# Weaving the convolution's norm, the past pages and half of the output projection into the prompt attention, with the value pages on SyncE's queue

## The reference: what is computed

```python
z = h @ W['w_in_even'][e]
q, k, v, fl, a, b = jnp.split(z, cuts, axis=-1)
logf = log_sigmoid(fl + b_forget)
o_fox = fox_attend(e, q, k, v, logf)          # prompt: causal; samples: 8 pages of 128 old tokens each
u = a * sigmoid(b)
xp = concatenate([conv_buf, u], axis=1)
cv = depthwise_conv(xp, conv_w) + conv_b       # 31 taps
cv = silu(_group_norm(cv, 8) * g + b)
out = concatenate([o_fox, cv], axis=-1) @ W['w_out_even'][e]
```

## Time and profile before

| | us |
|---|---|
| median of 3 runs (lowest, highest) | 1930.45 (1929.25, 1932.46) |
| the profiled execution, device time | 1925.21 |
| its span, first to last instruction | 1923.4 |
| PE busy | 1774.2 (92%) |
| DVE busy | 864.9 (45%) |
| ACT busy | 573.5 (30%) |
| POOL busy | 213.7 (11%) |
| mean granted clock of TensorE | 0.942 of 2.4 GHz |

### The profile page before, as it was taken

How to read it: one execution, slowest core, us unless ns; L and a number is a source line. 1 busy time by engine, 2 the same in 40 slices (tenths; PEclk the granted TensorE clock), 3 DMA queues, 4 the chain that set the end, 5 groups by cost and what they waited for, 6 DMA issues and landing times.

```text
span 1923.4 us, 31960 instructions
## 1 busy us (share of the span) xinstructions
PE 1774.2 (92%) x12929; PEld 1549.1 (81%) x12929; DVE 864.9 (45%) x1461; ACT 573.5 (30%) x816; POOL 213.7 (11%) x229
## 2 busy tenths in 40 slices
PE   5899888779899999999899999999968799999997
PEld 3899443327799999999797879799738799999997
DVE  2699346613533232334634637337463533333324
ACT  2422443201442122122333434314331432222223
POOL 1000048600200000000100101101120100000001
PEclk7899668789999999999999999999978999999998
DMA  8463045577434434443231725334742123233321
GB/s 300 139 214 102 2 138 153 175 256 236 147 94 164 149 103 146 144 139 97 66 105 53 224 76 185 121 91 135 263 141 86 58 88 99 77 97 97 89 72 53
DMA packets 288066, 248.82 MB, mean 129 GB/s; under 512 B 9000, under 2 KB 239816, under 8 KB 287951
## 3 DMA queue, kind: packets, MB, share of 16 engines
q1 hardware_dynamic: 262740, 173.97, 29.8%
q0 software_dynamic: 15824, 58.99, 8.6%
q10 hardware_dynamic: 9395, 14.36, 2.1%
HBM read 224.05 MB, written 23.70 MB: 129 GB/s over the span
## 4 chain that ended last, share of the span: by engine, by line
PE 83%; DVE 6%; ACT 3%; POOL 3%; DMA 2%; issue 2%; ACTq 1%; SPq 0%; POOLq 0%; DVEq 0%
PE product L728 60%; PE product L743 5%; PE job L1140 2%; POOL sqa L2094 2%; DMA vp<-in_cache_v 2%; PE job L625 2%; PE job L619 1%; PE job L1123 1%; PE job L917 1%; PE job L658 1%; PE job L893 1%; PE job L1026 1%; PE job L1115 1%; DVE rstd L1591 1%; PE job L1046 1%
## 5 line engine op out<-in xcount | busy, mean ns | idle before, releaser
L728 PE MATMUL product<-H_hi,w_lo 128*128 128x260 f32 x2368 | 674.1, 285 | 3.0 <-ACT gate L1172 2.9
L728 PE MATMUL product<-H_lo,w_hi 128*128 128x260 f32 x2368 | 668.9, 282 | 0.0
L728 PE MATMUL product<-H_hi,w_hi 128*128 128x260 f32 x2368 | 668.4, 282 | 0.0
L728 PEld LDWEIGHTS product<-H_hi,w_lo 128*128 128x128 f32 x2368 | 445.5, 188 | 16.2 <-issue 14.2
L728 PEld LDWEIGHTS product<-H_hi,w_hi 128*128 128x128 f32 x2368 | 446.1, 188 | 0.0
L728 PEld LDWEIGHTS product<-H_lo,w_hi 128*128 128x128 f32 x2368 | 445.9, 188 | 0.2
L1561 DVE TENSOR_TENSOR w_lo<-raw,w_hi 128x1024 fp32r<-128x1024 f32 (+1 forms) x228 | 274.9, 1207 | 169.1 <-ACT w_hi L1172 168.2
L1172 ACT ACTIVATE w_hi<-raw 128x1024 fp32r<-128x1024 f32 (+1 forms) x228 | 234.6, 1037 | 308.2 <-PE product L728 188.9
L728 PE MATMUL product<-G_hi,w_lo 128*128 128x260 f32 x912 | 260.4, 286 | 5.9 <-DVE X L1645 2.5
L728 PE MATMUL product<-G_lo,w_hi 128*128 128x260 f32 x912 | 259.3, 284 | 0.0
L728 PE MATMUL product<-G_hi,w_hi 128*128 128x260 f32 x912 | 259.2, 284 | 0.0
(11 more groups left out here) (319 smaller groups left out, 2139.3 us busy)
## 6 DMA issues: line engine op xcount, KB each, us to landing
spare<-in_ada_w POOLq DMA_DIRECT2D x24, 1024.0 KB, 9.0
raw<-in_w_in_odd SPq DMA_DIRECT2D x48, 512.0 KB, 3.7
raw<-in_w_ffn_gate SPq DMA_DIRECT2D x44, 512.0 KB, 3.8
raw<-in_w_ffn_up SPq DMA_DIRECT2D x44, 512.0 KB, 3.6
kp<-in_cache_k SPq DMA_DIRECT2D x64, 256.0 KB, 2.7
raw<-in_w_ffn_down SPq DMA_DIRECT2D x32, 512.0 KB, 3.3
st<-in_state_ret POOLq DMA_DIRECT2D x28, 512.0 KB, 4.3
out_ret_sample<-st POOLq DMA_DIRECT2D x28, 512.0 KB, 4.5
```

The costliest lines, as they stand in the source:

```text
L728: mm = pe.matmul(Gp[slot][:, c, 0:CH], w[:, j, k, :], x[:, k, cols], start=k == 0 and p == 0, stop=k == kt - 1 and p == 2)
```

## The change

Stages 2, 4, 5 and the convolution's half of stage 6 are put between the 32 steps of the attention. Tables of steps say which piece follows which step (`QB_AT`, `VN_AT`, `KN_AT`, `CM_AT`, `CB_AT`, `V_AT`, `GATHER_AT`, `CONV_OUT_AT`). In detail:

- The rows `cpo`, `cso`, `qs`, the running sums `cum` and `cumT`, the forget logs and the samples' taps go between the input blocks.
- Key pages: three per step instead of two, so that they end with step 21. The samples' softmax is made in two halves of four samples (steps 11 to 15 and 21 to 25).
- The group mean is subtracted by the matmul itself (a constant matrix of identity minus mean), and ACT writes the result and its square; the inverse root is spread with two matmuls of 64 rows each.
- The output projection is made as 8 blocks over the convolution's 512 features (`out_conv`, 24 matmuls each, steps 19 to 26) and 8 over the attention's 512 (`out_even`, 24 each, at the end). N_BLOCKS grows by 8; each block's weights have half the size.
- The values: 16 units of four pages in a ring of three units, laid in the halves of `raw`, `w_hi` that half-size blocks leave free, and in a third place. Two units make one sample; the result goes through a job (`ov`), ACT copies it, and the gather masks the heads through its right operand. All units are issued by SyncE, between the key pages; ScalarE issues none.
- Tiles are laid elsewhere (SS, kp, VN, sq4, lg and others) so that they can live at the same time.

```diff
+V_AT = {17: 0, 19: 1, 21: 2, 23: 3, 27: 4, 29: 5, 31: 6}
+CONV_OUT_AT = {19 + i: i for i in range(8)}
+PER_STEP = 3
...
-    jobs += [(("cm", t, c), "D") for t in range(4) for c in range(2)]
...
+            if x in CM_AT:
+                jobs += [(("cm", CM_AT[x], c), "A") for c in range(2)]
...
+        def value_unit(eng, u, js):
+
+            if u < 2:
+                eng.wait_ge(block_done, N_OUT_EVEN)
+                eng.wait_ge(lo_ready, N_OUT_EVEN)
+            elif u == 2:
+                wait_job(eng, ("cq", 1))
+            elif u % 2 == 0:
+                wait_job(eng, ("ov", (u - 3) // 2))
+            else:
+                eng.wait_ge(v_used, (u - 3) // 2 + 1)
+            for j in js:
+                page(eng, 4 * u + j, cache_v, value_page(u, j), v_unit[u % 3])
...
+            def centred(t):
+                pe.wait_ge(conv_step, 4 * CW)
+                pe.wait_ge(cs_ready, 4)
+                for c in range(2):
+                    bank = open_job(("cm", t, c))
+                    close(pe.matmul(bank[:, 0:CH], con[:, C_CEN:C_CEN + P], CV[:, t, c * CH:(c + 1) * CH],
+                                    start=True, stop=True))
...
+            def group_rstd(t):
+                pe.wait_ge(conv_act, 1)
+                for c in range(2):
+                    bank = open_job(("cb", t, c))
+                    for e in range(2):
+                        mm = pe.matmul(bank[HD * e:HD * e + HD, 0:CH],
+                                       con[0:8, C_ID + 2 * t + e:C_ID + 2 * t + e + 1].broadcast_to((8, HD)),
+                                       CR[:, c * CH:(c + 1) * CH], start=True, stop=True)
+                    close(mm)
...
+            def past_values(b):
+                bank = open_job(("ov", b))
+                pe.wait_ge(samp_dve, 7 + 5 * (b // 4))
+                for u in (2 * b, 2 * b + 1):
+                    pe.wait_ge(v_unit[u % 3], 64 * (u // 3 + 1))
+                    for j in range(4):
+                        mm = pe.matmul(bank[QD * j:QD * j + QD, :], weights_of(b, u % 2 * 4 + j), value_page(u, j),
+                                       start=u % 2 == 0, stop=u % 2 == 1)
+                    if u % 2 == 0:
+                        mm.then_inc(v_used, 1)
+                close(mm)
...
+            def conv_out(i):
+
+                n = N_OUT_EVEN + i
+                if i == 0:
+                    pe.wait_ge(g_ready, 4)
+                pe.wait_ge(lo_ready, n + 1)
+                slots_free(0, conv_base + i - 1)
+                product(n % 4, n % 2, 4, G_hi[:, 4:8], G_lo[:, 4:8]).then_inc(block_done, 1)
...
-            run("out_even", N_OUT_EVEN, 2, KD, G_hi, G_lo, "D")
+            run("out_even", N_OUT_EVEN + KD, 2, 4, G_hi, G_lo, "D")
...
-            act.wait_ge(v_stored, 16 * TB)
-            value_pages(act, 1)
...
-                    for g in range(2 * x, 2 * x + 2):
+                    for g in pages_of(x):
...
+            N = N_OUT_EVEN
+            key_pages(0, 4)
+            out_weights(N, N + 4)
+            key_pages(4, 20)
+            values(0, 2)
+            key_pages(20, 36)
+            values(2, 3)
+            key_pages(36, 52)
+            values(3, 5)
+            key_pages(52, 60)
+            values(5, 7)
+            out_weights(N + 4, N + 6)
+            key_pages(60, 64)
+            values(7, 9)
+            out_weights(N + 6, N + 8)
+            values(9, 11)
+            out_weights(N + 8, N + 12)
+            values(11, 16)
+            out_weights(N + 12, N + 16)
```

More of the change, by code:

```diff
@@ L57 @@
 N_OUT_EVEN = 20
-N_FFN = (28, 160)
-N_ODD = 96
-N_BLOCKS = 228
+N_FFN = (36, 168)
+N_ODD = 104
+N_BLOCKS = 236
 HEAD_BLOCKS = 12
@@ L954, in _ @@
-            turned = open_job("ov")
-            def weights_of(b, g):
-                first = b * PAGES + g
-                return SCP[:].rearrange("p h b g -> p (h b g)")[:, first:first + 31 * 16 + 1:16]
-            def gather(b):
-                pe.wait_ge(vm_ready, b + 1)
-                for t in range(4):
-                    mm = pe.matmul(turned[:, t * NB + b:t * NB + b + 1], vm[:, b % 2, t * P:(t + 1) * P],
-                                   one_col, start=True, stop=True)
-                return mm
@@ new lines, in gather @@
+            def gather(b):
+                bank = open_job(("og", b))
+                wait_emptied(pe, ("ov", b))
+                for t in range(4):
+                    mm = pe.matmul(bank[:, 2 * t:2 * t + 2], vm[:, b % 2, t * P:(t + 1) * P],
+                                   con[:, C_OWN + 2 * t:C_OWN + 2 * t + 2], start=True, stop=True)
+                close(mm)
+            conv_base = runs["out_conv"][1]
+            def conv_out(i):
[5 more added lines that the diff above has]
+                product(n % 4, n % 2, 4, G_hi[:, 4:8], G_lo[:, 4:8]).then_inc(block_done, 1)
@@ L1299, in stage_out @@
                 stage[s] += 1
-            act.wait_ge(cv_ready, 4)
-            stage_out("cpo", CW - 1, 512, A["conv_prompt"][0, 0])
-            stage_out("cso", NB, 512, A["conv_sample"][0, :, CW - 2, :])
-            wait_job(act, "qs")
-            n.up(f(qsn[:], Jp[jobs.bank("qs")][0:NB, :], ACT.Copy), emptied["A"])
-            for b in range(NB):
-                wait_job(act, ("qb", b))
-                n.up(f(QB[:, b, :], Jp[jobs.bank(("qb", b))][:, :], ACT.Copy, scale=FOX_SCALE), emptied["A"])
@@ new lines, in _ @@
+                    if x in EXP_AT:
+                        past_add(EXP_AT[x])
+                    if x in DN_AT:
+                        past_scale(DN_AT[x])
+                    if x in GATHER_AT:
+                        gather(GATHER_AT[x])
+                    if x == SILU_AT + 1:
+                        for t in range(4):
+                            dve.wait_ge(ghi_ready, t + 1)
+                            n.up(minus_hi(G_lo[:, 4 + t, :], CV[:, t, :], G_hi[:, 4 + t, :]), g_ready)
+                        lo(N_OUT_EVEN)
+                        lo(N_OUT_EVEN + 1)
```

821 lines of the change are left out of this document (496 added, 325 removed).

## The result

The changed kernel takes 1911.0 us, the median of 4 runs (1908.0 to 1914.1), beside 1930.9 us (1929.3 to 1932.5) of the kernel before in the same session: ratio 0.9897, 95% interval 0.9878 to 0.9916. It is 20 us faster, where 41 were forecast. Its profiled execution spans 1906.2 us, that of before 1923.4. Medians in this document are of fast runs, which leaves out one run of experiment 10 (its mean clock was 0.638, that of the others 0.943 to 0.949).

A forecast was written before the change was run, and what follows sets the result against it. It took a string of thin, serial stages from 196.8 to 498.2 us, with 51.5 us of TensorE idle, as the bound. Gains of 22.3 us (weave) and 18.8 (projection's rest) made 41, hence 1889 us; range 1848 to 1922.

The forecast's parts named there:

- the clock of the thin matmuls ahead of the blocks: Old attention's part of the weave: granted clock rises from 0.71 to 0.80, cutting 140 us of TensorE work to 124.
- the stall at key page 60: Units 5, 6 ahead of key page 60 in SyncE's queue: 0 us reaches TensorE, covered by some 21 us of work.
- Input projection, start of the weave: Input projection grows by 4.5 us, so the weave starts at 201.3 us instead of 255.2.
- The halves of the group rows: Group rows (L859) become two 64-row halves in the weave: 3.3 us more TensorE work, between 0 and 6.6.
- Value pages: Value pages in the weave wait in units of four: 24.2 us of TensorE work instead of 38.3.
- Projection blocks in the weave: Eight convolution-half blocks of 24 matmuls enter the weave: 8 x 2.97 = 23.8 us of TensorE work.
- SyncE's stalls: Value pages queued ahead of key pages 20, 36, 52, 60 idle TensorE 2, 4, 10, 0 us: 16 in all.
- Handshakes and tail: TensorE idle in the weave: 10 us waiting for banks, copies and softmax turns, 9 us at the last value unit.
- The projection's rest: From the output projection's second half to the mean's matmuls: 29.8 us instead of 48.6, a gain of 18.8.
- rival 2: Loose weave: clock 0.71, idle near today's, 252 us for the weave, 1915 us; chance 0.15.
- Rival 4: No effect: SyncE's queue order lets all four stalls reach TensorE, 43 us instead of 16; 1932 us; chance 0.03.
- Rival 3: Slower: small gaps keep the weave's clock low, losing below a mean of 0.72; 1975 us at 0.6; chance 0.07.

The follow-up runs named there:

- experiment 10: Convolution gates split between steps 16 and 17, on the changed kernel with value pages interleaved and a denser tail: 1870.8 us, ratio 0.9698.
- experiment 2: The interleaved kernel: changed kernel with SyncE's value pages issued singly between key pages instead of in bursts; 1886.3 us, ratio 0.9762.
- Experiment 4: Changed kernel without key-page loads, POOL's 64 products and DVE's 64 sums over them: 1880.9 us, ratio 0.9734.
- experiment 8: Eight extra dense, unused matmuls in each of steps 1 to 16, on top of experiment 2: 1893.7 us, ratio 0.9799.
- experiment 5: Changed kernel with the projection's eight convolution blocks moved out of steps 19 to 26, behind the last head's values: 1921.2 us, ratio 0.9946.
- Experiment 11: Changed kernel with only value units 5 and 6 moved, behind key page 63 instead of 59: 1903.9 us, ratio 0.9857.
- experiment 12: Changed kernel with only value units 3 and 4 moved, behind key page 55 instead of 51: 1900.3 us, ratio 0.9839.
- experiment 9: Changed kernel with all value-page bursts from unit 2 to 6 kept whole but four key pages later in SyncE's queue: 1892.0 us, ratio 0.9804.

## Why the prediction was right or wrong

It forecast 1889 us and got 1911. The sign was right and the time lies in the range, but the gain was half. Two steps failed: the clock of the thin matmuls ahead of the blocks, and the stall at key page 60, put at nothing. The place of the other stalls was right.

- **Input projection, start of the weave.** Forecast 201.3, measured 202.2. Right.
- **The halves of the group rows.** I took 3.3 us; they cost nothing. The 32 matmuls of 64-row tiles (L1014, 6.4 us in the trace) take what the 16 of the earlier trace rows took (6.6). The rule of the Trainium skill, "TensorEngine Tiling (Array Packing)", Key Properties, holds here.
- **Value pages.** Forecast 24.2 us, measured 19.8: units of four pages took 1.04 to 1.10 us where the clock was high (steps 19 to 21) and 1.9 where it was low (step 17), against the 1.51 us of the earlier trace rows.
- **Projection blocks in the weave.** Forecast 23.8, measured 29.1. Six of the eight blocks took 3.1 us each; the second took 4.7 and the fourth, right behind TensorE's wait of 3.1 us at 376.86, took 5.5. In experiment 2, without the stalls, steps 20 to 23 ran at 1.00.
- **Clock: the first step that failed.** "With the idle gaps filled and dense 128-row products between, the clock should be higher": 0.80 for the old attention's part. Everything but value pages and blocks took 150 us where 143 were forecast, at 0.72 up to step 24. Experiment 4 filled the gaps and got 0.75; dense work moved it further (experiment 8). The half of the reason that names dense products holds: from step 20 on the clock was 0.82 and 0.81, and without the blocks 0.59 and 0.70 (experiment 5, 14.6 us for the same work). But the blocks enter at step 19, behind most of the attention, so they could not lift the steps before, at 0.72, 0.64 and 0.67. The earlier trace rows had said so: 0.50 with TensorE 19.86 of 20 us busy. Taken together TensorE's work was 8 us over the forecast.
- **SyncE's stalls: right in sum, wrong in one.** Forecast 2, 4, 10 and 0 us at pages 20, 36, 52 and 60, together 16; the idle times give 1.5, 6.9, 6.7 and 4.9, together 20. The zero was the second step that failed: "PE has blocks 0 to 2 of the projection and unit pair 2, some 21 us". The cover was about right: from unit 5's first page (353.25) to the turn at 376.86 TensorE had 18.7 us of work. What was too short is the chain set against it. I took 13 to 14 us until the first product and 3.8 for three products, 17.5; these end at 370.96, after 17.7. Behind them I had left out DVE, which sums page 62, makes a w_lo, updates X for a block, takes the maximum of a score block, sums page 63 and takes the samples' maximum, until 376.71: 23.5 us in all, 4.8 over the cover, and 4.9 is what TensorE idled. Experiment 11 gives 7 us for this stall alone, and experiment 12 shows that it doesn't hang on the stall before.
- **Handshakes and tail.** Forecast 10 and 9; the interleaved kernel, without stalls, shows 14.3 before step 24 and 10.9 behind it. Idle in all: 44.8, not 35.
- **The projection's rest.** Forecast 29.8, measured 31.0 (at 0.89), and 1.6 us more in the mean's matmuls. I had allowed for this clock loss and not put it in the sum.
- **Sum.** Start 0.9 late, work 8, idle 9.8: 18.7 us at the fox half. Then 1.2 in the half, and 3.9 given back behind it, of which the mean's matmuls are 1.6: 23.8, the difference between the 41 forecast and the 17.2 that the two profiled executions show.
- **Rivals.** What came is rival 2, the loose weave, nearly number for number: clock 0.71 and idle 45 there, 0.73 and 44.8 here, 1915 against 1911. I gave it 0.15. Its reason (every engine carries more per step) is not what experiments 2 and 9 show: the same load per step runs at 25 and 32 us of idle. Rival 4 named the place, SyncE's queue, but at 43 us instead of 20. Rival 3 would need a mean clock under 0.72 over the whole weave; 0.73 was close to it, though the time was not: that sum took the blocks and value pages at full speed as 67 us, so its 0.72 is not the granted clock of the stretch (the forecast's own sum implies 0.87 and names "near 0.8" as its sign). I had also read the earlier trace rows as bearing out that waits lower the clock in the attention; it doesn't, since TensorE is busy 19.86 of 20 us there at 0.50.
- **Signs.** Four of them held: the start at 201, POOL's waits of 12.1 and 13.9 us at pages 36 and 52, TensorE dry behind step 18, and 24.8 us of TensorE's work in the fox half. Missed: TensorE 82% busy instead of over 85, its clock 0.73 instead of 0.8, the wait at page 20 (5.1 us, not 8), the 9.6 us at page 60, key pages done after 173 us instead of 140, the fox half at 446, the mean's matmuls at 477 instead of 457.

The change as it stands wins 20 us of 60 that its idea holds: the order of one queue was worth 25 more, the places of the last values and of four blocks, with their weights, another 16.

## What to carry to other kernels

When two streams share a queue, price the wait at the head of a burst before its issue time, and put the burst behind the entry at which its condition is already true: here that moved 19 us with the same bursts, 15 of them idle time between steps 12 and 23. When you call a stall hidden, follow it past the page that it delays to the last answer that the busy engine needs: the one at key page 60 looked covered until DVE's work behind the products was counted. And expect little clock from filling gaps between thin matmuls (0.72 to 0.75 here); look at what the clock is in a stretch that is already full, and at where the dense products stand, since here they lifted the clock of what stood between them.

## What the runs showed of the hardware

- The clock level follows the kind of work. Eight dense matmuls a step, 24 us in all, gave 0.79 where the other twelve kernels of the weave had 0.67 to 0.73 (experiment 8); steps 20 to 23 had 0.82 with dense blocks and 0.59 without (experiment 5). The Trainium skill, "TensorE: Matmul & The Clock Gate", HAM oscillation, tells of a fall by waiting between short bursts; here and the first pieces above show it low while TensorE is full.
- The same work ran at different clocks. TensorE's matmuls of steps 0 to 11 (240 of them) took 79.0 us at 0.72 in the changed kernel, 83.9 at 0.67 in experiment 2, and 70.6 at 0.80 in experiment 9, which up to key page 36 has the changed kernel's order:
```profile
204.70:282.73 78.03, 70.60 (x240) 37.86 (x239) 47.52 (x103) 34.25 (x86) 54.59 (x53) 0.80 0.60 173
```
  The difference is there from the start: from 204.7 to 214 us experiments 8 and 9 were granted 0.93, the changed kernel and experiment 2 0.50, with TensorE busy all the time in each. What sets it stays open. A comparison of two profiles of such a stretch is good to some 10 us; idle times are steadier.
- Pages issued by two queues at once land later: 4.0 to 4.8 us in the median for ScalarE's, 3.0 to 3.5 for SyncE's value pages beside them, 2.9 to 3.0 with SyncE alone.
